# A scan's turn as sixteen products of 64x64 tiles instead of four whole transposes

## The reference

```python
def wkv7_scan(r, w, k, v, a, b):
    def step(state, inp):
        r_t, w_t, k_t, v_t, a_t, b_t = inp
        sa = jnp.einsum('bhij,bhj->bhi', state, a_t)
        state = (state * w_t[:, :, None, :] + sa[..., None] * b_t[:, :, None, :]
                 + v_t[..., None] * k_t[:, :, None, :])
        y_t = jnp.einsum('bhij,bhj->bhi', state, r_t)
        return state, y_t
    _, ys = lax.scan(step, state0, xs)
    return jnp.moveaxis(ys, 0, 1)
```

## Time and profile before

| | us |
|---|---|
| median of three runs | 2260.97 (2260.62 to 2261.11) |
| the profiled execution | 2260.91 |
| its span in the trace | 2259.1 |
| scan, levels of t=0 (866.3 to 894.0) | 27.70 |
| scan, levels of t=1 (909.9 to 936.4) | 26.50 |

### The profile page before, as it was taken

One profiled execution on the slowest core, in us unless ns is written; L12 is line 12 of the kernel. 1 busy time (PEld: TensorE's weight loads), 2 busy tenths in 40 slices (PEclk: granted clock), 3 DMA queues, 4 the chain that ended last, 5 costly groups with the idle time before them and its releaser, 6 DMA issues.

```text
span 2259.1 us, 33177 instructions
## 1 busy us (share of the span) xinstructions
PE 2235.1 (99%) x13419; PEld 1824.6 (81%) x13419; DVE 1468.1 (65%) x2086; ACT 1156.4 (51%) x1674; POOL 181.1 (8%) x286
## 2 busy tenths in 40 slices
PE   9999999999999999999999999999999999999998
PEld 8888888887888758888887888878888788868887
DVE  6656757656765877676567656656656765677655
ACT  5445545445544464254455445465445544565444
POOL 1001001001000110410011001001001100051001
PEclk9999999999999999999999999999999999999999
DMA  8556656554755640065556555525555555526553
GB/s 275 186 186 215 214 168 200 187 178 167 225 183 193 206 144 12 29 209 184 186 194 195 185 188 195 174 94 164 186 186 195 182 183 188 196 76 201 186 178 111
DMA packets 290441, 395.58 MB, mean 175 GB/s; under 512 B 11848, under 2 KB 193424, under 8 KB 290288
## 3 DMA queue, kind: packets, MB, share of 16 engines
q1 hardware_dynamic: 285280, 377.13, 50.6%
q0 software_dynamic: 4720, 16.20, 2.0%
q10 hardware_dynamic: 288, 0.13, 0.0%
HBM read 392.37 MB, written 1.05 MB: 174 GB/s over the span
## 4 chain that ended last, share of the span: by engine, by line
PE 95%; DVE 2%; ACT 1%; issue 1%; POOL 0%; DMA 0%; DVEq 0%; POOLq 0%; ACTq 0%
PE bank L518 28%; PE bank L522 28%; PE bank L520 28%; PE bank L546 2%; PE bank L534 1%; PE bank L2583 0%; PE bank L1472 0%; PE bank L477 0%; PE bank L2577 0%; ACT JUNK L656 0%; PE bank L2594 0%; PE bank L1987 0%; PE bank L2554 0%; PE bank L1209 0%; ACT wh L649 0%
## 5 line engine op out<-in xcount | busy, mean ns | idle before, releaser
L839 DVE TENSOR_TENSOR wl<-raw,wh 128x1024 fp32r<-128x1024 f32 (+1 forms) x714 | 859.5, 1215 | 544.5 <-ACT wh L649 543.8
L649 ACT ACTIVATE wh<-raw 128x1024 fp32r<-128x1024 f32 (+1 forms) x714 | 745.8, 1052 | 636.9 <-PE bank L522 616.4
L518 PE MATMUL bank<-wh,XH 128*128 128x512 f32 x2000 | 799.0, 399 | 0.0
L520 PE MATMUL bank<-wl,XH 128*128 128x512 f32 x2000 | 780.3, 390 | 0.3 <-DVE wl L839 0.3
L522 PE MATMUL bank<-wh,XL 128*128 128x512 f32 x2000 | 780.1, 390 | 0.2 <-DVE XL L862 0.2
L518 PEld LDWEIGHTS bank<-wh,XH 128*128 128x128 f32 x2000 | 375.6, 188 | 83.6 <-issue 8.9
L522 PEld LDWEIGHTS bank<-wh,XL 128*128 128x128 f32 x2000 | 375.6, 188 | 81.9 <-DVE XL L862 0.7
L520 PEld LDWEIGHTS bank<-wl,XH 128*128 128x128 f32 x2000 | 376.1, 188 | 74.1 <-DVE wl L839 1.1
L518 PE MATMUL bank<-wh,AH 128*128 128x512 f32 x704 | 276.0, 392 | 0.0
L522 PE MATMUL bank<-wh,AL 128*128 128x512 f32 x704 | 274.1, 389 | 0.0
L520 PE MATMUL bank<-wl,AH 128*128 128x512 f32 x704 | 274.0, 389 | 0.0
(11 more groups left out here) (342 smaller groups left out, 1735.2 us busy)
## 6 DMA issues: line engine op xcount, KB each, us to landing
raw<-in_ffn_w_dram SPq DMA_DIRECT2D x178, 512.0 KB, 4.7
raw<-in_ffn_wi_dram SPq DMA_DIRECT2D x176, 512.0 KB, 4.6
raw<-in_ffn_w_dram SPq DMA_DIRECT2D x40, 1024.0 KB, 5.0
raw<-in_ffn_wo_dram SPq DMA_DIRECT2D x40, 1024.0 KB, 4.9
raw<-in_a_wqkv_dram SPq DMA_DIRECT2D x18, 1024.0 KB, 5.0
raw<-in_a_w_in_dram SPq DMA_DIRECT2D x16, 1024.0 KB, 5.1
raw<-in_b_w_in_dram SPq DMA_DIRECT2D x12, 1024.0 KB, 5.0
bc<-in_norm_g_dram POOLq DMA_DIRECT2D x16, 512.0 KB, 5.4
```

Of the source, the lines that this page charges most:

```text
L518: pe.e.matmul(o, a, h, start=(k == 0), stop=False)
L520: pe.e.matmul(o, a, l, start=False, stop=False)
L649: act.e.activation(self.wh[j % N_W][:, c0:c1], self.raw[p.chunk % N_RAW][:, p.at + c0:p.at + c1], ACT.Copy).then_inc(*self.rounded.up(*key))
L839: dve.e.tensor_tensor(self.wl[j % N_W][:, c0:c1], self.raw[p.chunk % N_RAW][:, p.at + c0:p.at + c1], self.wh[j % N_W][:, c0:c1].bitcast(F3 ...
```

## The change

The turn of Y in `pe_scan_level_a` is made of 16 products of 64x64 tiles with the unit matrix, in both banks of the pair, where four whole transposes into one bank were. ACT's copy reads the two banks. `scl` moves from between `level_a` and `level_b` to behind `level_b`. The lines of PE's scan up to the turn carry numbers smaller by three now (`pe_scan_decays` 2520, `pe_scan_krv` 2564), the turn is line 2576, lines 2583 to 2713 keep theirs, and those behind are larger by one.

```diff
@@ scan_steps
         for lv in range(1, 6):
-            steps += [("level_a", 0, 0, lv), ("level_a", 0, 1, lv)]
+            steps += [("level_a", 0, 0, lv), ("level_a", 0, 1, lv), ("level_b", 0, 0, lv), ("level_b", 0, 1, lv)]
             if lv < 5:
-                steps += [("scl", lv - 1)]
-            steps += [("level_b", 0, 0, lv), ("level_b", 0, 1, lv)]
-            if lv < 5:
-                steps += [("complete", lv)]
+                steps += [("scl", lv - 1), ("complete", lv)]
             if lv >= 4:
                 steps += [("tt", 1, lv - 4)]
@@ pe_scan_level_a
-        bank, _ = self.scan_pair(pe, ("x", t, o, lv), (self.moved, "x", t, o, lv))
+        banks = self.scan_pair(pe, ("x", t, o, lv), (self.moved, "x", t, o, lv))
         pe.wait_ge(self.made, "y", t, o, lv - 1)
         pe.wait_ge(self.made, "l", t, o)
         for r in range(4):
-            m = pe.e.transpose(bank[:, r * P:(r + 1) * P], Y[:, r, :, :].rearrange("p x n -> p (x n)"), self.ident[:, :])
+            for e, x in self.UNITS:
+                h = self.HALF[e]
+                m = pe.e.matmul(banks[e][self.HALF[x], r * HD:(r + 1) * HD], Y[h, r, x, :], self.ident[h, h], start=True,
+                                stop=True)
@@ act_rwkv_scan
-                act.e.activation(self.sX[o][:, :, :], self.scan_banks("x", t, o, lv)[:, 0:512].rearrange(
-                    "p (r n) -> p r n", r=4), ACT.Copy).then_inc(*self.moved.up("x", t, o, lv))
+                act.e.activation(self.sX[o][:, :, :].rearrange("p r (e n) -> p e r n", e=2), self.scan_banks(
+                    "x", t, o, lv).rearrange("p (e c) -> p e c", e=2)[:, :, 0:256].rearrange(
+                        "p e (r n) -> p e r n", r=4), ACT.Copy).then_inc(*self.moved.up("x", t, o, lv))
```

## The result

The changed kernel takes **2275.98 us** (median; the profiled execution 2272.54, span 2270.7) against 2260.97 before: ratio 1.0057, with its interval 1.0043 to 1.007. It is slower by about 15 us where 2258.4 was predicted. Run again beside the experiments (e16_after) it takes 2275.31 us against 2260.89, ratio 1.0065 [1.0049, 1.0082].

What follows compares the result with a forecast made beforehand. TensorE, busy in 99% of the span, was taken as the bound. Savings of 0.74 us in the first token tile and 1.82 in the second, 2.56 together, took 2260.91 to 2258.35, predicted as 2258.4 (2257.4 to 2259.6).

Steps and rivals of the forecast that it cites:

- part 1: Scan levels: turning Y by 64x64 products saves 0.39 us of TensorE order, 0.52 where the change into transposes goes too.
- x costs 0.46 where it cost 0.59: Turn of Y in a block: 32 small passes at 0.014 us take 0.46 us, four transposes took 0.59.
- rival D: Slower: the turn's new passes don't run four abreast; at the two-corner step of 0.032 us, 2266.2 us; chance 0.07.
- Slower: Whole kernel: outcome above 2265.5 us; chance 0.05.
- point of decision of 0.022 us: Turn of Y: step per pass at which two blocks cost what is saved in a level.
- The rule of the Trainium skill: Turn of Y: about 60 cycles overhead per product, 25 ns, so 0.80 us a turn and 2262.4 us.
- Neither clock nor memory plays a part in the scan: Scan: granted clock 1.00 and DMA queues at only 3 to 4 GB/s, so only TensorE time counts.
- Part 2: First token tile: decays' products behind the last products gain 0.69, 0.92, 1.24 us in levels 1 to 3, finally 0.74.
- Level 1 of t=1: Second token tile, first level: second half's last products start 2.66 us after the first turn, against 3.05 before.
- The copies of W on DVE: Scan: VectorE's copies of the product of Y with L hold the last products, and move with earlier work.
- The walk of 0.17 us: Scan blocks: TensorE's idle time going back from a whole transpose to 64x64 tiles, 0.17 us, saved ahead of the product with L.

Runs made afterwards that it cites:

- e16_after: The changed kernel, with nothing altered, run once more beside the experiments; 2275.31 us against 2260.89 for the kernel before, ratio 1.0065.
- e9_chain: Kernel before plus unread chains: 512 small four-corner products before the first levels, 160 transposes at t=1; first chain ran 128 passes per 3.73 to 4.0 us.
- e10_chain: Kernel before plus unread chains: 256 small two-corner products at t=0, 80 whole f32 products at t=1; the first chain's 512 passes took 15.0 us.
- e13_waits: Kernel before plus 1120 already-satisfied TensorE wait instructions in the scan, 14 ahead of each transpose; 2382.3 us.
- e14_fewer: Kernel before plus 560 already-satisfied TensorE wait instructions in the scan, 28 in each turn; 2321.69 us.
- e15_linear: Kernel before plus 1120 already-satisfied TensorE waits in a linear layer, two ahead of each three 128x512 products; 2261.01 us, ratio 1.0002.
- e8_second: Changed kernel with the turn by products only in the second token tile, old transposes in the first; 2267.34 us, ratio 1.0023.
- e4_whole: Kernel before with each transpose of the turn replaced by a whole 128x128 f32 product, two passes instead of one; 2278.44 us, single run.

## Why the prediction was wrong

- **The step that failed** is the first of part 1: "x costs 0.46 where it cost 0.59". Its size in the array was right: 0.46 to 0.54 us from x to w at full clock, and none of the two-corner pitch of rival D. But 0.46 came from a single group of 32 passes, and I carried it to 192 passes in a row in every level. I counted passes as time in the array, and not as instructions that must arrive. The supply gives a pass every 0.029 to 0.031 us (e9_chain), so the 192 passes of a level need 5.6 us or more where no stock is left, where a level of t=1 before took 3.9 (x0 at 928.81 and at 932.71). In the profile after the last three levels begin at 932.87, 937.33 and 941.84 and end at 948.53: 4.5, 4.5 and 6.7 us, 5.2 on the mean.
- **The rivals.** Slower had a chance of 0.05. D had the right sign, and 0.030 us is beyond its point of decision of 0.022 us for a pass, but that was luck: its reason, passes that don't run four abreast, is wrong (32 passes in 0.46 to 0.54 us between the stops), and its 2266.2 is still 10 us short. The trace of before had a sign of it: the instruction packets, 23 in 98 us, close to one per 4 us, and one idle time "issue" at 860.8 of 0.78 us in the products just ahead of the scan. I did not read that queue.
- **The rule of the Trainium skill** (TensorEngine Tiling, Instruction Overhead; don't tile what is small) pointed the right way, to 2262.4, and I set it aside by the row of 0.014 us. The row was right and what I drew from it was not. The overhead for each product, which the rule rests on, is not what cost time: between the stops the passes went as the row says.
- **The clock.** "Neither clock nor memory plays a part in the scan" held for the kernel before, not for the one after: 0.88 to 0.94 in the stretches, worth 5 to 7 of the 15 us by the estimate above, and at most 7.2 of 14.4 by the rows of e16_after.
- **Part 2**, the decays, was right in its reasoning (a gain in levels 1 to 3, given back in level 4) and too large in its gain: in e2_decays, which has the move alone, 0.2 us by the end of level 3 where 1.24 was forecast for the move with the new turn, and with the loss in level 4 the last `pe_decay` comes 0.3 us later than before, not 0.74 earlier.
- **Level 1 of t=1.** w0, x1 and w1 begin 0.49 us apart (916.18, 916.67, 917.16), close to the 0.46 of the forecast, but w1 stops for its instructions and goes on at 917.83. W1's copy on DVE is late by that (918.28), and b1 starts 0.13 after its end, at 918.83, which is 3.4 us after x0 (915.41) and not 2.66. The copies of W on DVE, on which most terms of the sum hung, still hold b, by 1.5 us in the whole scan; what they leave is taken by the supply.
- **The walk of 0.17 us** back from a whole tile was taken for a price of the array's change of form. At b, the idle time behind W falls from 0.9 to 0.4 us when the wait instruction goes, so about half of it was that instruction's. The 0.17 ahead of w, which the prediction priced, no run took apart.

## What to carry to other kernels

Before a few large instructions of TensorE are replaced by many small ones, count them as instructions: passes in a stretch, times two, against the 256 per 3.7 to 4.0 us that arrive here. A pitch read from one short group is the array's, and holds only while that stock lasts. A stall in the middle of a group, put down to "issue" and repeated at one distance, is the sign. If the only cover of such a stage is its high granted clock, look after the change whether it is still granted.

## What the runs showed of the hardware

- TensorE got 256 instructions per 3.73 to 4.0 us, and no more, once its stock was used up (e9_chain, a single run; 3.6 to 4.0 between the stops of the kernel after); 512 passes of 0.029 us are just not slowed (e10_chain). An f32 product is two passes, four instructions.
- A wait instruction of its own on TensorE costs 0.108 us when the array has no long product to cover it (e13_waits, e14_fewer), nothing behind products of 0.39 us (e15_linear).
- The granted clock fell to 0.50 for some 3 us at a time in the profile after, and was below 0.997 on the mean in all eight of its undisturbed runs; in the kernel before it was so in one to four of the 12 to 27 runs beside each set of experiments, and these took 6 to 8 us more. What brings it down stays open: stalls are in most of the cases (the kernel after, e8_second, e13_waits) but not in e4_whole, and in e9_chain the clock stayed full with the stalls and was at half for 24 us behind them.
- How much of the 15 us is stalls and how much the clock was not separated by a run; 8 to 10 and 5 to 7 is the best estimate, and the rows of e16_after leave the clock at most half.
